# Pooling bands moved in the load queue, gate rows and weight loads tied to later work in a two-block transformer kernel

## The chip, the cores and the metric

The kernel runs on one core of a Trainium2 chip. A core has a matrix engine (TensorE, PE in the profile, with PEld for its weight loads), a vector engine (VectorE, DVE), a scalar engine (ScalarE, ACT), GpSimd (POOL) and a sync engine (SyncE, SP) that here does nothing but issue loads. Each engine runs its own list of instructions in the order in which they are written and waits on semaphores. 16 DMA engines carry the loads. Loads that SP issues, those that ACT issues and those that POOL issues form three queues (q1, q10 and q0). The metric is the device time of one execution in microseconds (us); lower is better.

## The reference, cut to what matters

Two transformer blocks of two layers each run on 256 tokens of 1024 features, all in float32. The changed code is in the first layer of the first block:

```python
def sandwich(x, mod, g_pre, g_post, fn):
    shift, scale, gate = mod                     # split(silu(c) @ ada_w + ada_b, 3)
    h = rms_norm(x, g_pre) * (1.0 + scale[:, None]) + shift[:, None]
    return x + gate[:, None] * rms_norm(fn(h), g_post)

def mixer(h, j=j):                               # layer 0
    u, qr, fr, vr, gr = jnp.split(h @ hyb_w_in[j], split_at, axis=-1)
    y = jnp.concatenate([pool_mixer(u, pool_w[j], pool_scale[j]),
                         hgrn2_mixer(qr, fr, vr, gr, lower_bounds[j], hgrn_out_norm[j])], axis=-1)
    return y @ hyb_w_out[j]
```

`pool_mixer` takes a windowed mean over the tokens minus the token itself (in the kernel a matmul with a table of bands), then a 128x128 weight per group. `hgrn2_mixer` is a gated linear recurrence with q = silu(q_raw); the kernel computes it by levels that double in length. Behind the mixer come a feed-forward layer (swiglu), then the second layer (dilated attention, swiglu), then the second block.

## The kernel before, in words

Each float32 weight matmul is done as three products of a high and a low part. Weights come in loads of 1 MB into a ring of six slots (`raw`). A load has two halves; the `split` of ACT casts a half to its high part (`whi`, L587), the `split` of DVE subtracts it (`wlo`, L1373, which raises `lo_ready`), and TensorE multiplies. There are four slots of high and low parts.

The start, up to about 147 us of the profile, is made of these steps:

- Eight modulation chunks of 1 MB and four loads of hyb_w_in (half of which hold two blocks each) alternate in SP's queue. DVE makes the shift and scale of the first norm from the chunks; each chunk done raises `ada_used`. TensorE multiplies block 0 (pooling inputs u) and block 1 (the forget gate) as eight tiles.
- Six loads n4 to n9 (hyb_in 4 to 9) hold blocks 2 (query), 3 and 4 with halves 8 to 19; four loads n10 to n13 hold hyb_w_out with halves 20 to 27; n14 is the first load of the feed-forward layer with halves 28 and 29. In the code, `split(2 * FIRST["hyb_in"] + 14 + i)` is half 14 + i.
- TensorE runs halves 8 and 9, then the eight pooling matmuls with `bandqk` (which wait for `band_in`, raised by the bands and by `poolw`, and for the copy of block 0 out of PSUM), halves 10 and 11, then eight levels of the recurrence with one half ahead of each.
- ACT copies the blocks out of PSUM (`evac`), makes sigmoids and Silu, prepares keys, and in each level makes the level copies (L922, L923), which DVE's next level and TensorE's scores wait for.
- DVE makes the query product `QG` (L1793), the level products, the masked merges (`copy_predicated` with `masks`) and the splits; between them stand items of work on rows: 8 gate items (`gate_items(0, ...)`, one row of the gate weights of the first mixer each) and 16 items of the second modulation (`col_items(1, ...)`). Each item raises `ada_step`.
- POOL issues the rows, 0.5 MB each, into a ring of four (`ada_ring`); a row is issued once the item four places back is done. The first gate row waits for `ada_used`.
- Two semaphore waits of SP hold back the loads. Load n of 4 to 13 waits for `lo_ready` of 2 * (n - EARLY) + 2, and n14 waits for the count of one of the four row semaphores:

```python
if isinstance(it, int) and max(EARLY, len(HYB_AT)) <= n < FIRST["ffn0"]:
    sp.wait_ge(s["lo_ready"], 2 * (n - EARLY) + 2)
...
sp.wait_ge(ada_in[3], 16 * 5)
```

The fourth row semaphore (`ada_in[3]`) counts rows 3, 7, 11, 15, 19 and 23 of the whole sequence; the rows 8 to 23 of that sequence are rows 0 to 15 of the second modulation.

Of the kernel before, what the change touches and what calls it, by code (L numbers as in the profile page):

```python
# [47 lines left out]
FIRST, _n = {}, 0  # L48
ADA_FIRST = 8
# [1 line left out]
HYB_AT = (1, 4, 7, 10)  # L51
ROW_STEP = 1
GATE_ITEMS, COL_ITEMS = (0, 24, 48, 72), (None, 8, 32, 56)
EARLY = 3
for _name, _k in PHASES:
    FIRST[_name] = _n
    _n += _k
# [35 lines left out]
def program(nc, t):  # L93

    with ExitStack() as ctx:
        s = {name: ctx.enter_context(nc.semaphore(name)) for name in SEMS}
        raw_in = [s[f"raw_in{i}"] for i in range(RAW)]
        ada_in = [s["ada_in0"], s["ada_in1"], s["ada_in2"], s["ada_in3"]]
# [95 lines left out]
        def flat(bank, n=2):  # L194
            return ps[:, bank:bank + n, :].rearrange("p a b -> p (a b)")
# [192 lines left out]
        def _(sp):  # L388
# [35 lines left out]
            def proj(n, w, blocks, it=0, step=0):  # L424
                for b, (_, col0, _) in enumerate(blocks):
                    for kh in range(2):
                        load(n + 2 * b + kh, it, src_cols(w, col0 + step * it, kh))
# [26 lines left out]
            for at in range(ADA_FIRST + len(HYB_AT)):  # L454
# [3 lines left out]
                    load_both(HYB_AT.index(at))  # L458
                if at == 2:
                    sp.dma_start(voh[:, :], t["voh"]).then_inc(s["const_in"], 16)  # L460
            proj(FIRST["hyb_in"] + 4, t["hyb_w_in"][0], HYB[2:])
            for c in range(4):
                load(FIRST["hyb_out"] + c, 0, src_down(t["hyb_w_out"][0], c * 2 * P))
            sp.wait_ge(ada_in[3], 16 * 5)
            swiglu(FIRST["ffn0"], 0)
            with sp.Fori(0, 2) as i:
                proj(FIRST["qkv"], t["att_w_qkv"][0], QKV_B, i, 1536)
# [23 lines left out]
        def _(pool):  # L491
# [33 lines left out]
            pool.memset(gg[:, :, :], 0.0).then_inc(s["gg_zero"], 1)  # L525
            bias_row(0)
            bias_row(1)
            pool.wait_ge(s["ada_used"], ADA_FIRST - 1)
            gate_rows(0, range(8))
            gain_row(0)  # L530
            mod_rows(1, range(16))
# [43 lines left out]
        def _(act):  # L575
            A = nc.scalar

            def split(H, it=0):

                if isinstance(it, int) and H >= HALVES:  # L580
                    return
                n, h = H // 2, H % 2
                if h == 0:
                    act.wait_ge(raw_in[slot(n)], in_count(n) + 16 * it)
                if H >= 4:
                    act.wait_ge(s["pe_used"], H - 3 + 12 * it)
                A.copy(whi[:, H % 4, :], raw[:, slot(n), h * HALF:(h + 1) * HALF]).then_inc(s["hi_ready"], 1)  # L587
# [261 lines left out]
            for k in range(KD):  # L849
                split(k)  # L850
                if k == 5:
                    table_row(0)
                    table_row(1)
                if k == 7:
                    act.dma_start(bandqk[:, :], t["band"]).then_inc(s["band_in"], 16)
                    act.dma_start(poolw[:, :, :], t["pool_w"][0].rearrange("g c d -> c g d")).then_inc(s["band_in"], 16)
                if k == 0:
                    act.wait_ge(s["turned"], KD)
                act.wait_ge(s["mod_ready"], k + 1)
                if k >= 4:  # L860
                    act.wait_ge(s["hlo_ready"], k - 3)
                A.activation(h32_slot(0, k), turned_ps(0, k), ACT.Identity, bias=shcol[:, 0, k:k + 1],
                             scale=scol[:, 0, k:k + 1])
                A.activation(hhi[:, k, :], turned_ps(0, k), ACT.Identity, bias=shcol[:, 0, k:k + 1],
                             scale=scol[:, 0, k:k + 1]).then_inc(s["hhi_ready"], 1)
                if k == 6:
                    table_row(2)
                    act.wait_ge(s["vec_dil"], 3 + DG)
                    A.copy(vrow[:, 3 * VLEN_DIL:], ps[0:8, 5, :]).then_inc(s["vec_dil_c"], 1)
                    act.wait_ge(s["vec_dil_c"], 4)  # L870
                    act.dma_start(t["vec_dil"].rearrange("g h n -> h g n"),
                                  vrow[:, 0:3 * VLEN_DIL].rearrange("h (g n) -> h g n", g=3)).then_inc(s["vec_out"], 16)
                    act.dma_start(t["vec_swa"], vrow[:, 3 * VLEN_DIL:]).then_inc(s["vec_out"], 16)
# [3 lines left out]
            fl = f1[:, :, :].rearrange("p a b -> p (a b)")  # L877
            split(8)
            split(9)
            evac(0, KD, "A", HYB[0][2], f1, tok1)  # L880
            act.dma_start(masks[:, :, :], t["masks"]).then_inc(s["cols_in"], 16)
            evac(1, KD, "B", HYB[1][2], f1, tok1)
            split(10)
            split(11)
            act.wait_ge(s["vec_out"], 32)
            act.wait_ge(s["proj_free"], 2)
# [9 lines left out]
            for h in range(HL):  # L896
# [2 lines left out]
                ins = A.activation(fl[:, 1024 + a:1024 + a + S], fl[:, 1024 + a:1024 + a + S], ACT.Identity,  # L899
                                   bias=small[:, 4, h:h + 1], scale=small[:, 4, 4 + h:5 + h])  # L900
            ins.then_inc(s["hg_prep"], 1)
            evac(2, 2 * FIRST["hyb_in"] + 12, HYB[2][0], HYB[2][2], f1, tok1)
            act.wait_ge(s["proj_free"], 3)
            A.activation(fl[:, 0:1024], fl[:, 0:1024], ACT.Silu).then_inc(s["sig_ready"], 1)
            A.copy(pooled[:, :, :].rearrange("p a b -> p (a b)"), flat(6)).then_inc(s["pool_dc"], 1)
            split(13)
            split(14)
            split(15)
# [448 lines left out]
        def _(dve):  # L1357
# [244 lines left out]
            def proj(name, blocks, at=0, it=0):  # L1602
                for b in range(len(blocks)):
                    for q in range(4):
                        split(2 * (FIRST[name] + 2 * (at + b)) + 4 + q, it)
# [181 lines left out]
            split(11)  # L1787
            gate_items(0, acc_a, (1,))
            split(12)
            gate_items(0, acc_a, (2, 3))  # L1790
            dve.wait_ge(s["hg_prep"], 1)
            dve.wait_ge(s["sig_ready"], 3)
            V.tensor_tensor(QG, fl[:, 0:1024], fl[:, 1024:2048], ALU.mult).then_inc(s["hg_prep"], 1)  # L1793
            gate_items(0, acc_a, (4,))
            split(13)
            split(14)

# [39 lines left out]
            for i in range(8):  # L1837
                if i:
                    level(i)
                if 0 <= i - 1 < 5:  # L1840
                    merge(i - 1)
                if i:
                    split(2 * FIRST["hyb_in"] + 14 + i)
                if 1 <= i <= 3:
                    gate_items(0, acc_a, (i + 4,))
                elif 4 <= i <= 6:
                    col_items(1, (i - 4,))
                if i == 7:
                    dve.wait_ge(s["hyb_hi"], 1)
                    V.tensor_tensor(hlo[:, 0:4, :], y1[:, 0:4, :], hhi[:, 0:4, :].bitcast(F32), ALU.subtract) \  # L1850
                        .then_inc(s["hyb_lo"], 1)
            split(2 * FIRST["hyb_in"] + 22)
            col_items(1, (3, 4))
            split(2 * FIRST["hyb_in"] + 23)
            col_items(1, (5, 6))
            split(2 * FIRST["hyb_out"] + 4)
            col_items(1, (7, 8))
            dve.wait_ge(s["sig_ready"], 4)
            for c in range(2):
                yv = y1[:, 4 + 2 * c:6 + 2 * c, :].rearrange("p a b -> p (a b)")  # L1860
# [7 lines left out]
                V.tensor_tensor(hlo[:, 4 + 2 * c:6 + 2 * c, :], y1[:, 4 + 2 * c:6 + 2 * c, :],  # L1868
                                hhi[:, 4 + 2 * c:6 + 2 * c, :].bitcast(F32), ALU.subtract).then_inc(s["hyb_lo"], 1)
            split(2 * FIRST["hyb_out"] + 5)  # L1870
            col_items(1, (9, 10))
            split(2 * FIRST["hyb_out"] + 6)
            col_items(1, (11,))
            split(2 * FIRST["hyb_out"] + 7)
            col_items(1, (12, 13))
            whole_gate(0, 2)
            col_items(1, (14, 15))
            split(2 * FIRST["hyb_out"] + 8)
            renew(1)
            split(2 * FIRST["hyb_out"] + 9)  # L1880
# [1393 lines left out]
```

## Time and profile before

| | |
|---|---|
| Time, median of 3 runs | 1264.63 us (1264.23 to 1266.15) |
| The profiled execution | 1264.12 us, span 1262.3 us |
| TensorE busy | 1233.4 us, 98% of the span |
| VectorE busy | 920.2 us, 73% |
| ScalarE busy | 721.1 us, 57% |
| Mean granted TensorE clock | 0.995 of full speed |
| HBM read | 272.30 MB, 217 GB/s over the span |

The busy shares are averages over all stages. In the first 150 us the three compute engines and the queues have other shares than later, and the change is there.

### The profile page before, as it was taken

How to read it: one execution, taken by the hardware profiler on the slowest of the kernel's cores; microseconds unless marked ns; L12 is line 12 of the kernel's file. 1: busy time of each engine (PE TensorE's matmuls, PEld its weight loads, DVE VectorE, ACT ScalarE, POOL GpSimd, SP SyncE). 2: the span in 40 equal slices, each digit the busy share in tenths (PEclk: the TensorE clock that was granted, in tenths of full speed). 3: DMA queues.
4: the chain of work that ended last, by engine and by line, in shares of the span. 5: the costliest groups of instructions: out<-in, count | busy, mean ns of one | idle time of the engine just before them, and what ended most of it. 6: DMA issues, size and time to landing. Idle time of an engine off the chain costs nothing.

```text
span 1262.3 us, 20465 instructions
## 1 busy us (share of the span) xinstructions
PE 1233.4 (98%) x7874; PEld 1118.5 (89%) x7874; DVE 920.2 (73%) x1193; ACT 721.1 (57%) x1062; POOL 63.1 (5%) x116
## 2 busy tenths in 40 slices
PE   8799899999999999999999999999999999999999
PEld 6698799999899778999989989888888888888888
DVE  7779878886897558666676695676666777766665
ACT  5676644444744557444466664665555667655554
POOL 1101111110121000000001000000000000000000
PEclk9999899999999999999999999999999999999999
DMA  9967989995699624666656544356666552466650
GB/s 362 395 223 254 340 304 328 330 331 195 242 384 392 210 48 167 200 200 199 199 167 214 165 152 151 131 201 201 201 205 202 188 171 92 131 214 203 200 167 34
DMA packets 145903, 274.39 MB, mean 217 GB/s; under 512 B 5463, under 2 KB 86383, under 8 KB 145704
## 3 DMA queue, kind: packets, MB, share of 16 engines
q1 hardware_dynamic: 130524, 220.50, 51.8%
q0 software_dynamic: 14256, 50.94, 11.4%
q10 hardware_dynamic: 1052, 1.97, 0.4%
q8 instruction: 48, 0.79, 0.3%
q14 instruction: 23, 0.19, 0.0%
HBM read 272.30 MB, written 1.10 MB: 217 GB/s over the span
## 4 chain that ended last, share of the span: by engine, by line
PE 86%; DVE 6%; DMA 3%; ACT 2%; issue 2%; SPq 0%; ACTq 0%; DVEq 0%
PE ps L2321 85%; DVE wlo L1373 2%; DMA raw<-in_hyb_w_in 1%; DMA poolw<-in_pool_w 1%; ACT whi L587 1%; PE ps L2763 1%; DVE raw L1401 1%; DMA ada_ring<-in_ada_t 1%; DVE ada_ring L1401 0%; DVE h L1476 0%; DVE x L1485 0%; PE ps L2487 0%; PE ps L2500 0%; DVE rs L2041 0%; DVE prob L1998 0%
## 5 line engine op out<-in xcount | busy, mean ns | idle before, releaser
L1373 DVE TENSOR_TENSOR wlo<-raw,whi 128x1024 fp32r<-128x1024 f32 x400 | 488.4, 1227 | 241.0 <-ACT whi L587 240.3
L587 ACT CAST whi<-raw 128x1024 fp32r<-128x1024 f32 x400 | 417.3, 1050 | 402.3 <-PE ps L2321 386.9
L2321 PE MATMUL ps<-hboth,whi 128*128 128x256 f32 (+1 forms) x2720 | 605.3, 311 | 0.7 <-DVE hboth L1597 0.2
L2321 PE MATMUL ps<-hboth,wlo 128*128 128x256 f32 x1792 | 491.3, 274 | 0.6 <-DVE wlo L1373 0.2
L2321 PEld LDWEIGHTS ps<-hboth,whi 128*128 128x128 f32 x2720 | 448.0, 191 | 29.9 <-issue 5.3
L2321 PEld LDWEIGHTS ps<-hboth,wlo 128*128 128x128 f32 x1792 | 344.2, 192 | 2.9 <-issue 1.0
L2321 PE MATMUL ps<-whi,hboth 128*128 128x512 f32 (+1 forms) x520 | 158.0, 374 | 9.3 <-DVE hboth L1427 7.1
L2321 PE MATMUL ps<-whi,hidhi 128*128 128x512 f32 (+1 forms) x436 | 164.8, 378 | 0.0
L2321 PE MATMUL ps<-wlo,hidhi 128*128 128x512 f32 (+1 forms) x436 | 164.4, 377 | 0.0
L2321 PE MATMUL ps<-whi,hidlo 128*128 128x512 f32 (+1 forms) x436 | 164.4, 377 | 0.0
L2321 PEld LDWEIGHTS ps<-whi,hboth 128*128 128x128 f32 x520 | 96.8, 190 | 26.6 <-issue 12.8
L2321 PE MATMUL ps<-wlo,hboth 128*128 128x512 f32 (+1 forms) x260 | 94.9, 365 | 0.0
L2321 PEld LDWEIGHTS ps<-wlo,hidhi 128*128 128x128 f32 x436 | 82.5, 189 | 11.5 <-issue 0.2
L2321 PEld LDWEIGHTS ps<-whi,hidlo 128*128 128x128 f32 x436 | 82.4, 189 | 11.5
L2321 PEld LDWEIGHTS ps<-whi,hidhi 128*128 128x128 f32 x436 | 82.6, 189 | 10.5 <-ACT whi L587 0.2
L1401 DVE CUSTOM_DVE_ANT_0 ada_ring<-ada_ring,scrow,cols 128x1024 f32<-128x1024 f32 x48 | 61.0, 1291 | 1.7 <-DMA ada_ring<-in_ada_t 1.5
L2321 PEld LDWEIGHTS ps<-wlo,hboth 128*128 128x128 f32 x260 | 49.5, 190 | 6.0 <-issue 1.0
L1720 DVE TENSOR_REDUCE tmp<-ps 128x512 f32<-128x1024 f32 x32 | 39.0, 1219 | 3.5 <-PE ps L2321 3.5
L1725 DVE TENSOR_TENSOR hidlo<-hid,hidhi 128x512 fp32r<-128x512 f32 x32 | 22.2, 692 | 16.7 <-ACT hidhi L810 16.7
L496 POOL DMA_DIRECT2D ada_ring<-in_ada_t x48 | 25.4, 530 | 134.7 <-DVE shcol L1401 63.6
L1394 DVE SCALAR_TENSOR_TENSOR acc_a<-ada_ring,sc,acc_a 128x1024 f32<-128x1024 f32 x21 | 27.3, 1298 | 0.5
L496 POOL DMA_DIRECT2D ada_ring<-in_ada_w x32 | 17.0, 531 | 140.0 <-DVE scol L1401 61.4
(271 smaller groups left out, 1120.7 us busy)
## 6 DMA issues: line engine op xcount, KB each, us to landing
raw<-in_ffn_w_in SPq DMA_DIRECT2D x44, 1024.0 KB, 5.5
raw<-in_w_mlp_up SPq DMA_DIRECT2D x32, 1024.0 KB, 5.3
raw<-in_w_mlp_down SPq DMA_DIRECT2D x32, 1024.0 KB, 4.9
ada_ring<-in_ada_t POOLq DMA_DIRECT2D x48, 512.0 KB, 6.0
raw<-in_ffn_w_out SPq DMA_DIRECT2D x22, 1024.0 KB, 4.9
raw<-in_att_w_qkv SPq DMA_DIRECT2D x18, 1024.0 KB, 8.9
raw<-in_w_in_even SPq DMA_DIRECT2D x18, 1024.0 KB, 5.1
ada_ring<-in_ada_w POOLq DMA_DIRECT2D x32, 512.0 KB, 6.5
```

The source lines that it names most:

```text
L496: pool.dma_start(ada_ring[:, l % 4, :], src).then_inc(ada_in[l % 4], 16)
L587: A.copy(whi[:, H % 4, :], raw[:, slot(n), h * HALF:(h + 1) * HALF]).then_inc(s["hi_ready"], 1)
L1373: V.tensor_tensor(wlo[:, H % 4, :], raw[:, slot(n), h * HALF:(h + 1) * HALF], whi[:, H % 4, :].bitcast(F32), ALU.subtract).then_inc(s["lo_ ...
L1394: ins = V.scalar_tensor_tensor(out=acc[:, :], in0=row, scalar=sc[:, k:k + 1], in1=acc[:, :], op0=ALU.mult, op1=ALU.add)
L1401: return V.tensor_tensor_reduce(out=row, in0=row, in1=scrow[:, :], scale=1.0, scalar=col(name, 8 * j + k), op0=ALU.mult, op1=ALU.add, accu ...
L1720: V.tensor_reduce(in_order(tmp2[:, g % 3, :], 2), parts_of(UP_BANK[g % 3]), AX, ALU.add) \
L1725: V.tensor_tensor(hidlo2[:, g % 3, :], hid2[:, g % 3, :], hidhi2[:, g % 3, :].bitcast(F32), ALU.subtract).then_inc(s["mhid_lo"], 1)
L2321: return pe.matmul(out, lhsT, rhs, start=first, stop=last, skip_group_check=True)
L2763: m = pe.transpose(dl_turned(p, i)[:, (j - j0) * P:(j - j0 + 1) * P], dl_block(p, j), ident[:, :])
```

## The change

The diff does seven things: (1) the loads of the bands and of pool_w go from ACT's queue to SP's, directly behind the last modulation chunk; (2) the load of the masks goes from ACT's queue to SP's, behind n5; (3) EARLY is 2 in place of 3; (4) n14 waits for a count of 6 rows in place of 5; (5) POOL's first gate row waits for eight chunks used in place of seven; (6) ACT casts half 10 ahead of the copies of blocks 0 and 1, and makes the pooled copy ahead of the copy of block 2 and of the Silu; (7) DVE has gate items 2 to 5 ahead of the query product and item 6 behind it, and all later items of the second modulation two places earlier, with `whole_gate` behind the last of them.

```diff
-EARLY = 3
+EARLY = 2
@@ sync
-            proj(FIRST["hyb_in"] + 4, t["hyb_w_in"][0], HYB[2:])
+            sp.dma_start(bandqk[:, :], t["band"]).then_inc(s["band_in"], 16)
+            sp.dma_start(poolw[:, :, :], t["pool_w"][0].rearrange("g c d -> c g d")).then_inc(s["band_in"], 16)
+            proj(FIRST["hyb_in"] + 4, t["hyb_w_in"][0], HYB[2:3])
+            sp.dma_start(masks[:, :, :], t["masks"]).then_inc(s["cols_in"], 16)
+            proj(FIRST["hyb_in"] + 6, t["hyb_w_in"][0], HYB[3:])
...
-            sp.wait_ge(ada_in[3], 16 * 5)
+            sp.wait_ge(ada_in[3], 16 * 6)
@@ gpsimd
-            pool.wait_ge(s["ada_used"], ADA_FIRST - 1)
+            pool.wait_ge(s["ada_used"], ADA_FIRST)
@@ scalar
-                if k == 7:
-                    act.dma_start(bandqk[:, :], t["band"]).then_inc(s["band_in"], 16)
-                    act.dma_start(poolw[:, :, :], t["pool_w"][0].rearrange("g c d -> c g d")).then_inc(s["band_in"], 16)
...
             split(9)
+            split(10)
             evac(0, KD, "A", HYB[0][2], f1, tok1)
-            act.dma_start(masks[:, :, :], t["masks"]).then_inc(s["cols_in"], 16)
             evac(1, KD, "B", HYB[1][2], f1, tok1)
-            split(10)
...
             ins.then_inc(s["hg_prep"], 1)
+            A.copy(pooled[:, :, :].rearrange("p a b -> p (a b)"), flat(6)).then_inc(s["pool_dc"], 1)
             evac(2, 2 * FIRST["hyb_in"] + 12, HYB[2][0], HYB[2][2], f1, tok1)
...
-            A.copy(pooled[:, :, :].rearrange("p a b -> p (a b)"), flat(6)).then_inc(s["pool_dc"], 1)
@@ vector
-            gate_items(0, acc_a, (2, 3))
+            gate_items(0, acc_a, range(2, 6))
...
-            gate_items(0, acc_a, (4,))
+            gate_items(0, acc_a, (6,))
...
-                if 1 <= i <= 3:
-                    gate_items(0, acc_a, (i + 4,))
-                elif 4 <= i <= 6:
-                    col_items(1, (i - 4,))
+                if i == 1:
+                    gate_items(0, acc_a, (7,))
+                elif 2 <= i <= 6:
+                    col_items(1, (i - 2,))
...
             split(2 * FIRST["hyb_out"] + 5)
-            col_items(1, (9, 10))
+            col_items(1, (11, 12))
             split(2 * FIRST["hyb_out"] + 6)
-            col_items(1, (11,))
+            col_items(1, (13,))
             split(2 * FIRST["hyb_out"] + 7)
-            col_items(1, (12, 13))
+            col_items(1, (14, 15))
             whole_gate(0, 2)
-            col_items(1, (14, 15))
```

What stands on ACT before, from the cast of half 8 to the sigmoids (L587 is a cast, tok is block 0, f is block 1):

```order
L587 CAST whi<-raw 128x1024 [waits pe_used,raw_in0]
L587 CAST whi<-raw 128x1024 [waits pe_used]
L597 COPY tok<-ps 128x2x512 [waits pe_used]
L881 DMA masks<-in_masks 128x1024
L595 COPY f<-ps 128x1024 [waits pe_used]
L587 CAST whi<-raw 128x1024 [waits pe_used,raw_in1]
L587 CAST whi<-raw 128x1024 [waits pe_used]
L887 ACT_TABLE_LOAD [waits proj_free]
L887 ACTIVATE sq<-f 128x1024 [waits vec_out]
```

And in the changed kernel (L591 is the cast there):

```order
L591 CAST whi<-raw 128x1024 [waits pe_used,raw_in0]
L591 CAST whi<-raw 128x1024 [waits pe_used]
L591 CAST whi<-raw 128x1024 [waits pe_used,raw_in1]
L601 COPY tok<-ps 128x2x512 [waits pe_used]
L599 COPY f<-ps 128x1024 [waits pe_used]
L591 CAST whi<-raw 128x1024 [waits pe_used]
L887 ACT_TABLE_LOAD [waits proj_free]
L887 ACTIVATE sq<-f 128x1024 [waits vec_out]
```

The cast that waits for n5 (`raw_in1`) stands now ahead of the two copies of blocks, and the load of the masks is gone from ACT.

What stands on SP in the changed kernel from the last modulation chunk to the first feed-forward load:

```order
L400 DMA raw<-in_ada_t 128x2x1024 [waits ada_used]
L461 DMA bandqk<-in_band 128x2048
L462 DMA poolw<-in_pool_w 128x4x128
L422 DMA raw<-in_hyb_w_in 128x4x512 [waits ada_used,lo_ready]
L422 DMA raw<-in_hyb_w_in 128x4x512 [waits lo_ready]
L464 DMA masks<-in_masks 128x1024
L422 DMA raw<-in_hyb_w_in 128x4x512 [waits ada_used,lo_ready] x2
L422 DMA raw<-in_hyb_w_in 128x4x512 [waits lo_ready]
L422 DMA raw<-in_hyb_w_in 128x4x512 [waits ada_used,lo_ready]
L422 DMA raw<-in_hyb_w_out 128x2x1024 [waits lo_ready] x4
L422 DMA raw<-in_ffn_w_in 128x8x256 [waits lo_ready,ada_in3]
```

Before, the loads of hyb_w_in followed each other without the three rows of L461, L462 and L464; the values waited for are in the diff.

What stands on DVE before, behind the last low part ahead of the hyb_out halves (L1401 is an item of the second modulation, L1451 is `whole_gate`):

```order
L1868 TENSOR_TENSOR hboth<-y,hboth 128x512 [waits hyb_hi] x2
L1373 TENSOR_TENSOR wlo<-raw,whi 128x1024 [waits hi_ready]
L1401 ISA ada_ring,scol<-ada_ring,scrow,cols 128x1024 [waits ada_in1]
L1401 ISA scol 128x1
L1401 ISA ada_ring,scol<-ada_ring,scrow,cols 128x1024 [waits ada_in2]
L1401 ISA scol 128x1
L1373 TENSOR_TENSOR wlo<-raw,whi 128x1024 [waits hi_ready]
L1401 ISA ada_ring,scol<-ada_ring,scrow,cols 128x1024 [waits ada_in3]
L1401 ISA scol 128x1
```

And in the changed kernel at the same place:

```order
L1868 TENSOR_TENSOR hboth<-y,hboth 128x512 [waits hyb_hi] x2
L1373 TENSOR_TENSOR wlo<-raw,whi 128x1024 [waits hi_ready]
L1401 ISA ada_ring,scol<-ada_ring,scrow,cols 128x1024 [waits ada_in3]
L1401 ISA scol 128x1
L1401 ISA ada_ring,scol<-ada_ring,scrow,cols 128x1024 [waits ada_in0]
L1401 ISA scol 128x1
L1373 TENSOR_TENSOR wlo<-raw,whi 128x1024 [waits hi_ready]
L1401 ISA ada_ring,scol<-ada_ring,scrow,cols 128x1024 [waits ada_in1]
```

The items behind half 25's low part are 9 and 10 before (rows of the semaphores `ada_in1` and `ada_in2`) and 11 and 12 now (`ada_in3` and `ada_in0`).

## Rows read from the trace of the kernel before

**Rows 1.** The page: the span, and TensorE's busy time and share.

```profile
span 1262.3 us, 20465 instructions
PE 1233.4 (98%) x7874; PEld 1118.5 (89%) x7874; DVE 920.2 (73%) x1193; ACT 721.1 (57%) x1062; POOL 63.1 (5%) x116
```

**Rows 2.** Waits of TensorE: us in total, times, longest.

```profile
PE ps L2487 <- DVE xn L1523: 6.9, 3, 5.3
PE ps L2321 <- DMA poolw<-in_pool_w: 4.2, 1, 4.2
```

**Rows 3.** The chain that ended last: start, us, what.

```profile
146.66 73.52 PE ps L2321 x572
```

**Rows 4.** Window: length, busy of PE, PEld, DVE, ACT, POOL, clock, DMA, GB/s.

```profile
57.10:62.20 5.10, 5.04 (x17) 4.19 (x17) 3.70 (x3) 2.69 (x3) 1.49 (x3) 0.67 1.04 398
```

**Rows 5.** Timeline of SP and POOL: start, us, what is issued.

```profile
28.28 0.47 SPq L400 DMA_DIRECT2D raw<-in_ada_t  x1
...
73.73 0.37 SPq L422 DMA_DIRECT2D raw<-in_hyb_w_in  x1
...
117.28 0.53 POOL L496 DMA_DIRECT2D ada_ring<-in_ada_t  x1 [2.13 <-DVE shcol L1401]
...
121.81 1.07 SPq L422 DMA_DIRECT2D raw<-in_ffn_w_in  x2
```

**Rows 6.** DMA issues at 28, at 72 and from 75: KB, us to landing.

```profile
raw<-in_ada_t SPq DMA_DIRECT2D x1, 1024.0 KB, 11.4
...
raw<-in_hyb_w_in SPq DMA_DIRECT2D x1, 1024.0 KB, 6.2
...
raw<-in_hyb_w_out SPq DMA_DIRECT2D x3, 1024.0 KB, 5.0
```

**Rows 7.** Queues in windows 41-42, 43-44, 130-131: packets, MB, engine share.

```profile
q1 hardware_dynamic: 194, 0.39, 105.4%
...
q0 software_dynamic: 71, 0.29, 73.3%
...
q0 software_dynamic: 84, 0.31, 80.0%
q1 hardware_dynamic: 85, 0.09, 24.5%
```

**Rows 8.** ACT: a window as in rows 4, then its timeline.

```profile
50.88:70.03 19.15, 14.98 (x94) 13.64 (x94) 8.46 (x7) 13.40 (x18) 2.64 (x5) 0.91 0.94 352
...
68.97 1.06 ACT L904 ACTIVATE f<-f 128x1024 f32<-128x1024 f32 x1
...
76.86 0.85 ACT L923 COPY sq<-bandqk 128x512 f32<-128x512 f32 x1
...
104.01 1.01 ACT L595 COPY f<-ps 128x1024 f32<-128x1024 f32 x1 [0.78 <-PE ps L2321]
...
128.19 2.23 ACT L587 CAST whi<-raw 128x1024 fp32r<-128x1024 f32 x2 [4.67 <-DMA raw<-in_ffn_w_in]
```

**Rows 9.** Timeline of DVE: start, us, what, idle before and who ended it.

```profile
70.14 1.23 DVE L1793 TENSOR_TENSOR bandqk<-f 128x1024 f32<-128x1024 f32 x1 [8.75 <-ACT f L904]
...
80.69 1.00 DVE L1832 TENSOR_TENSOR bandqk<-pooled,tot 128x512 f32<-128x512 f32 x1
...
98.06 1.44 DVE L1401 CUSTOM_DVE_ANT_0 ada_ring<-ada_ring,scrow,cols 128x1024 f32<-128x1024 f32 x1
...
106.00 1.23 DVE L1850 TENSOR_TENSOR hboth<-y,hboth 128x1024 fp32r<-128x1024 f32 x1 [0.45 <-ACT hboth L947]
...
124.61 1.28 DVE L1401 CUSTOM_DVE_ANT_0 ada_ring<-ada_ring,scrow,cols 128x1024 f32<-128x1024 f32 x1
...
132.10 1.28 DVE L1401 CUSTOM_DVE_ANT_0 ada_ring<-ada_ring,scrow,cols 128x1024 f32<-128x1024 f32 x1 [1.53 <-DMA ada_ring<-in_ada_t]
...
139.64 0.75 DVE L1485 SCALAR_TENSOR_TENSOR x<-h,small,x 128x512 f32<-128x512 f32 x1
...
143.89 0.75 DVE L1523 TENSOR_SCALAR xn<-x,small 128x1024 f32<-128x1024 f32 x1
```

More of the change, by code:

```diff
@@ L1852, in _ @@
             split(2 * FIRST["hyb_in"] + 22)
-            col_items(1, (3, 4))
+            col_items(1, (5, 6))
             split(2 * FIRST["hyb_in"] + 23)
-            col_items(1, (5, 6))
+            col_items(1, (7, 8))
             split(2 * FIRST["hyb_out"] + 4)
-            col_items(1, (7, 8))
+            col_items(1, (9, 10))
             dve.wait_ge(s["sig_ready"], 4)
```

## The prediction

> **What bounds the kernel now.** I read the page first: TensorE is busy for 98% of the span of 1262.3 us [rows 1], so time can only come from its few idle stretches or go into new ones. Then its waits: one of 4.2 us for the pooling weights and one of 5.3 us for the normalised x ahead of the first feed-forward stage [rows 2]. Everything the change touches ends before 147 us, and behind that point the chain that ends last stays on TensorE for 73.5 us on end [rows 3], so whatever shift the first feed-forward stage receives is carried to the end one for one. Then the windows: in 57.1 to 62.2, with the eight pooling matmuls, TensorE has a granted clock of 0.67, a mixture of its two levels (1.2 and 2.4 GHz), after the 4.2 us of standing idle [rows 4]. Last, the queues and the other two engines, which run in written order: a load that is late stops ScalarE (ACT) at its cast, and all that is written behind the cast waits too.
>
> Names: n4 to n13 are the one-block weight loads of SP (six of hyb_w_in, four of hyb_w_out), n14 is the first of ffn_w_in. Load n holds halves 2n and 2n+1, each cast by ACT and then subtracted by VectorE (DVE).
>
> **Part 1: bands and pooling weights ahead of n4.** The last modulation chunk was issued at 28.28 and landed 11.4 us later, at 39.7; the queue of SP is that deep [rows 5, 6]. Alone, that queue moves 0.39 MB per us [rows 7], window 41 to 42. Behind it stand now the bands (1.05 MB, 2.7 us), pool_w (0.26 MB, 0.7 to 0.9 us) and n4 (1.05 MB, 2.7 us): n4 lands at 45.9. Two passes (a cast of 1.05 on ACT, a subtraction of 1.15 on DVE) make its half 8 ready at 48.2, about when TensorE has finished the eighth tile: no more than 0.4 us lost. The pooling inputs land at 43.3, well ahead.
>
> But TensorE's pooling also needs the copy of PSUM block 0, and ACT now makes it behind the cast of half 10, so behind n5. From 39.7 on the engines must move the bands, pool_w, n4, four gate rows (4 x 0.52 MB, which start about 46) and n5: 5.5 MB at 0.39 is 14.1 us, so n5 lands at 53.8. That does not hang on how the two queues share, because the row queue takes 0.29 of 0.39 when both have work [rows 7], window 43 to 44, and is finished first. The cast (1.0 us) and copy (1.0 us) put pooling at 55.9, against 57.2 before; bounds 54.5 (rows late) and 56.5.
>
> The next thing late is ACT's query Silu, which the query product on DVE needs. From the cast of half 10 to the end of the Silu took 19.15 us before (50.88 to 70.03), with 13.4 us of work and the rest idle for a load and for TensorE [rows 8]; 13.5 with the small gaps. Now three copies more stand in that piece (blocks 0 and 1, and the pooled copy moved ahead of the Silu), 1.0 us each: 16.5 us. 53.8 and 16.5 is 70.3. The product started at 70.14 before [rows 9]. So the 4.2 us wait shrinks, and the slow clock behind it may go (5.04 us busy at 0.67 is 3.4 at full clock, some 1.6 us), but what follows from them is given back at once: the query product starts at the old time. Value of part 1: 0, between -0.8 (n5 at 53.0) and +0.5. The two further gate items moved into DVE's 8.75 us idle ahead of the product cost nothing there, since their rows (issued behind items 0 and 1, near 58 and 61) have until 69 to land; the masks are needed behind the first level and land behind n5, at 55.
>
> **Part 2: EARLY 3 to 2.** Each of n4 to n13 now waits for one load more to be split: n waits for half 2n-3 to be subtracted, before for half 2n-5. n8 was issued behind half 11; now it is issued behind half 13, where n9 was: 73.73. A load issued just there took 6.2 us with one row beside it, others 5.0 [rows 5, 6]. So n8 lands at 79.9 (78.8 to 80.2). Behind the cast of its half 16 (1.05 us) stand ACT's level copies 1 (1.7 us), the second of which ended at 77.7 before [rows 8]; now at 82.6. DVE's level 2 needs them and started at 80.69 [rows 9]: DVE is late by 1.9 us (0.8 to 2.2). DVE has no idle time of its own from there to half 21, so it keeps that. TensorE's levels had some 2 us in hand over DVE's merges and are late by 1.1.
>
> n11 is issued behind half 19 now, which ended where the next item begins, at 98.06 [rows 9], and ends at 100.0 (plus 1.9). It lands at 105.1 (5.0 us) or 106.2. What ACT has in its row then: cast of half 22 (1.0), level copies 7 (1.2), merge 6 (0.7), copy of block 4 (1.0): 109.0. The copy of block 4 ended at 105.0 before [rows 8] and the low part of the first four feature tiles, two steps behind, began at 106.00 [rows 9]. Late by 4.0 us, bounds 2.5 (1.9 replaced by 0.8, 5.0 kept) and 5.2. n10, n12 and n13 are late too, but stop ACT where nothing is waited for.
>
> **Part 3: the gate row count 5 to 6.** The rows and items of the second modulation are numbered 0 to 15 as in the code. n14 waits now for row 15, before for row 11. A row is issued when the item four places back is done. Row 11 followed item 7, and n14 was issued at 121.81 [rows 5]. From the issue of row 11 at 117.28 (0.4 behind the end of item 7) to n14's issue it took 4.5 us. Row 15 follows item 11, which now stands where item 9 stood, so ends at 124.61 [rows 9] plus 4.0 = 128.6. With the same 0.4 and 4.5, n14 is issued at 133.5.
> It landed 6.4 us after issue, when ACT's cast began at 128.19 [rows 8] and the row queue stood still for most of it. Now the four rows of the next gate and a gain row are issued beside it. When both have work, the row queue takes 0.31 MB per us and the 1 KB pieces of ffn_w_in 0.09, with 84 and 85 pieces each [rows 7], window 130 to 131; that would make it 10.3. I take 7.5, since the row queue has gaps of over 1 us between rows: 141.0. The Trainium skill, page "DMA: Bandwidth & Descriptors", section "Queues, rings and completion order", says that an engine takes turns between queues by whole packets of typically 9 to 17 descriptors; its section on SWDGE and HWDGE prefers packets up to 4096 B. Bytes would then be shared evenly, n14 would take about 6.5 and the time be 1 us less. The trace shows equal numbers of pieces and unequal bytes, so the sum goes by the trace.
>
> ACT has n14's two casts (2.2 us) ahead of the squares of y. Two squares (1.6) and the root (0.5) follow, 4.4 us with the gaps, then DVE's update of x, which before began at 139.64, and 4.25 us later the normalisation at 143.89 [rows 9]. So normalisation starts at 141.0 + 4.4 + 4.25 = 149.7: late by 5.8 us. Without the new wait DVE would have reached it at 143.9 even with the 4.0 us of part 2, because two modulation items fewer stand in that stretch (2.4 us) and the 1.53 us wait for a row [rows 9] goes. So the 4.0 and the 5.8 aren't added: the chain through the row, n14 and ACT contains the 4.0 and takes DVE's saving away. Bounds: with part 2 at 2.5 and n14 in 5.0 us it is 5.8 - 1.5 - 2.5 = 1.8; with part 2 at 5.2 and n14 in 10.3 it is 5.8 + 1.2 + 2.8 = 9.8.
>
> **Sum.** The profiled execution took 1264.12 us, span 1262.3. Plus 5.8 is 1269.9; the median of the runs stands 0.5 above the profiled one: 1270.4.
>
> **Rivals.**
> A, faster: n5 lands early enough that the copy of block 0 is not held up, by 50 or so. Then pooling runs at 53.4, TensorE is 5 us ahead, the query Silu comes some 3 us earlier, and DVE goes into the levels that much sooner. Every later load is tied to DVE's progress and moves too; with the two items fewer at the end it would be 3 to 4 us faster: 1261. It decides on n5's landing: below 51. Against it: 3.3 us too many bytes stand ahead of n5.
> B, no change: the late loads stop ACT but the waits die in slack, and n14 lands as fast as before (row queue idle). DVE's own row then sets the end: 0 to 1 us late, 1265.4. For it: DVE's path alone gives 0. Against it: ACT's casts stand ahead of the copies and squares in written order.
> C, worse: the waits at the levels and at hyb_out let the clock fall to 1.2 GHz, as after the 4.2 us at 57 [rows 4]; another 1.6 us as there, and n14 at its slow bound (2.8): 1274.8.
>
> **Chances.** Forecast 0.62 (own range 1267.3 to 1273), A 0.11, B 0.17, C 0.10. A measurement here can tell about 0.2%, 2.5 us. Faster by more than that: A, 0.10. Within: B, the edge of A and the low edge of the forecast, 0.20. Slower: 0.70. The 8-in-10 range takes B and most of C in: 1264.5 to 1274.
>
> **What would show it.** Right: no wait of TensorE for poolw, but one of 2 to 3 us at the same matmul put down to the copy of block 0; the query product at 70 to 71; ACT idle for hyb_w_in at half 16 (about 4 us) and for hyb_w_out at half 20 and 22; TensorE waiting 2 to 3 us near 107; ACT idle for ffn_w_in until about 141; the wait for the normalised x at 7 to 9 us. Wrong: level copies 1 finished before 80, or n14 landing before 137. If the pooling matmuls start before 54.5, step 1 is wrong and A gains.

## The result, and the profile after

The changed kernel takes 1276.39 us (median of 4 runs, 1275.4 to 1277.84) against 1264.64 us: the ratio is 1.0092, with a 95% interval of 1.0074 to 1.0109. The forecast was 1270.4. The profiled execution after took 1275.4 us with a span of 1273.5 us, against 1264.12 and 1262.3 [rows 1].

The page of the changed kernel, the span and the busy time of the engines:

```profile
span 1273.5 us, 20465 instructions
PE 1234.9 (97%) x7874; PEld 1119.9 (88%) x7874; DVE 920.6 (72%) x1193; ACT 718.1 (56%) x1062; POOL 62.9 (5%) x116
```

The busy time is the same within 2 us on every engine but ACT (3 us less), and the span is 11.2 us longer. The difference stands in waits. The waits of TensorE in the changed kernel, as in [rows 2]:

```profile
PE ps L2486 <- DVE xn L1523: 11.8, 3, 10.2
...
PE ps L2320 <- DVE wlo L1373: 3.8, 4, 1.7
PE ps L2320 <- ACT tok L601: 2.5, 1, 2.5
PE ps L2320 <- ACT sq L923: 1.8, 1, 1.8
```

The wait for the pooling weights has gone, and in its place stands one of 2.5 us for the copy of block 0 (`tok`), as forecast. The wait for the normalised x grew from 5.3 to 10.2 us, and small ones were added at the levels. The chain that ended last, as in [rows 3], from the hyb_out halves on:

```profile
109.23 0.02 ACT f L599
...
111.22 1.23 DVE hboth L1850
...
116.29 7.56 DMA ada_ring<-in_ada_t
...
130.46 1.20 DVE ada_ring L1401
131.67 0.28 issue
131.95 3.74 DMA ada_ring<-in_ada_t
135.71 11.72 DMA raw<-in_ffn_w_in
147.45 1.99 ACT whi L591 x2
...
155.91 0.68 DVE xn L1523
...
166.54 3.47 PE ps L2320 x29
```

It is the path of part 3, step by step: item 11 ends at 131.67, row 15 is issued and lands in 3.74 us, n14 is issued at 135.71 and takes 11.72 us, ACT casts it, and 8.4 us behind the landing x is normalised. On the timeline of DVE, as in [rows 9], all that went late is seen in turn:

```profile
70.71 1.22 DVE L1793 TENSOR_TENSOR bandqk<-f 128x1024 f32<-128x1024 f32 x1 [1.03 <-ACT f L905]
...
83.31 0.69 DVE L1832 TENSOR_TENSOR bandqk<-pooled,tot 128x512 f32<-128x512 f32 x1 [2.13 <-issue]
...
111.22 1.23 DVE L1850 TENSOR_TENSOR hboth<-y,hboth 128x1024 fp32r<-128x1024 f32 x1 [2.21 <-ACT hboth L947]
...
123.87 1.29 DVE L1401 CUSTOM_DVE_ANT_0 ada_ring<-ada_ring,scrow,cols 128x1024 f32<-128x1024 f32 x1 [1.67 <-DMA ada_ring<-in_ada_t]
...
155.82 0.75 DVE L1523 TENSOR_SCALAR xn<-x,small 128x1024 f32<-128x1024 f32 x1
```

Against [rows 9] the query product is late by 0.6, level 2 by 2.6, the low part ahead of hyb_out by 5.2, and the normalisation by 11.9 us (155.82 against 143.89). The span grew by 11.2: that shift, less 0.7 us that was not traced. The other three runs are up to 2.4 us longer than the profiled one; they left no traces.

### The profile page after: what moved, and what is told of

It reads as the page before. It is cut to its first block, busy times and chain, and to the rows that moved or that the text cites. A ratio compares the mean times of both kernels' runs of the same rounds, so it can differ in the third digit from the quotient of the medians.

```text
span 1273.5 us, 20465 instructions
## 1 busy us (share of the span) xinstructions
PE 1234.9 (97%) x7874; PEld 1119.9 (88%) x7874; DVE 920.6 (72%) x1193; ACT 718.1 (56%) x1062; POOL 62.9 (5%) x116
## 3 DMA queue, kind: packets, MB, share of 16 engines
q1 hardware_dynamic: 131340, 222.34, 51.7%
## 4 chain that ended last, share of the span: by engine, by line
PE 83%; DVE 6%; DMA 4%; ACT 4%; issue 2%; SPq 0%; ACTq 0%; DVEq 0%
PE ps L2320 82%; DMA raw<-in_hyb_w_in 3%; DVE wlo L1373 2%; ACT whi L591 1%; DMA raw<-in_ffn_w_in 1%; DMA ada_ring<-in_ada_t 1%; PE ps L2762 1%; DVE raw L1401 1%; DVE h L1476 0%; DVE x L1485 0%; PE ps L2486 0%; PE ps L2499 0%; DVE ada_ring L1401 0%; DVE rs L2040 0%; DVE prob L1997 0%
## 5 line engine op out<-in xcount | busy, mean ns | idle before, releaser
L591 ACT CAST whi<-raw 128x1024 fp32r<-128x1024 f32 x400 | 416.7, 1048 | 430.4 <-PE ps L2320 386.4
L2320 PEld LDWEIGHTS ps<-whi,hboth 128*128 128x128 f32 x520 | 97.7, 192 | 31.6 <-issue 16.5
L1401 DVE CUSTOM_DVE_ANT_0 ada_ring<-ada_ring,scrow,cols 128x1024 f32<-128x1024 f32 x48 | 60.6, 1280 | 1.9 <-DMA ada_ring<-in_ada_t 1.9
```

What stands on the lines that cost most here:

```text
L1401: return V.tensor_tensor_reduce(out=row, in0=row, in1=scrow[:, :], scale=1.0, scalar=col(name, 8 * j + k), op0=ALU.mult, op1=ALU.add, accu ...
L2320: return pe.matmul(out, lhsT, rhs, start=first, stop=last, skip_group_check=True)
```

## The experiments

Theory 1 is the path just read: EARLY 2 makes the weight loads late, the count of 6 puts n14 behind row 15, and the rows of the next gate that POOL issues beside n14 lengthen its landing. Its rivals are told with each run. All ratios are to the kernel before on the same chip, with 95% intervals. Its medians there were 1264.39 us (for the first four kernels below), 1265.14 (the next four), 1264.29 (the next two) and 1264.22 (the last).

**The count back to 5.**

```diff
-            sp.wait_ge(ada_in[3], 16 * 6)
+            sp.wait_ge(ada_in[3], 16 * 5)
```

> The changed kernel with n14's wait for row 11 again (count 5), all else as changed. Theory 1 (two costs: the loads tied one further back make the recurrence about 5 us late, and the count of 6 makes n14 land at 147.4, about 6 us more): n14 is issued at about 125.5 behind row 11 and lands by 137, so the normalised x comes at about 147 in place of 155.8; time 1267 to 1269. Theory 2 (the count costs nothing, all of it is EARLY): stays at 1276. Theory 3 (it is the count alone): back to 1264 or below.

1267.42 us (1265.76 to 1271.49), ratio 1.0024 (1.0014 to 1.0034). n14 is issued at 127.26 in place of 135.71 and x is normalised 7.0 us earlier:

```profile
148.82 0.75 DVE L1523 TENSOR_SCALAR xn<-x,small 128x1024 f32<-128x1024 f32 x1
```

So both costs of theory 1 are there. The count is worth 0.68% here (1.0092 against 1.0024) and 0.69% when it alone is added to the kernel before (below). It is not the largest single cost in the changed kernel: EARLY put back alone gives 0.82% (next).

**EARLY back to 3.**

```diff
-EARLY = 2
+EARLY = 3
```

> The changed kernel with EARLY 3 again, count still 6. Theory 1: halves 16, 20 and 22 are cast without a wait for their loads, the first hyb_out half starts at about 107.4 in place of 112.6, n14 is issued near 129 and still takes about 11 us, the normalised x comes at about 149; time 1269 to 1271. Theory 2 (EARLY is all of it): 1263 to 1265. Theory 3 (the count is all of it): stays at 1276.

1266.13 us (1261.92 to 1268.81), ratio 1.001 (0.9997 to 1.0023): better than expected by 3 us, and spread over 7 us. Two lines of ACT show one reason. The cast that waits for n5, in the changed kernel:

```profile
54.64 1.04 ACT L591 CAST whi<-raw 128x1024 fp32r<-128x1024 f32 x1 [6.55 <-DMA raw<-in_hyb_w_in]
```

And with EARLY 3:

```profile
51.93 1.05 ACT L591 CAST whi<-raw 128x1024 fp32r<-128x1024 f32 x1 [3.55 <-DMA raw<-in_hyb_w_in]
```

EARLY acts on n4 and n5 too; I had priced it only from n8 on. With EARLY at 2, n5 waits for the low part of half 7 and is issued at 44.20; with EARLY at 3 it waits for half 5 and is issued at 38.96, and it lands 2.7 us earlier. With EARLY 3 the pooling matmuls don't wait at all and the query product starts at 68.16, 2 us ahead of the kernel before. In this trace n14 is issued at 126.00 and takes 7.89 us. The spread is taken up below.

**Both back.**

```diff
-EARLY = 2
+EARLY = 3
...
-            sp.wait_ge(ada_in[3], 16 * 6)
+            sp.wait_ge(ada_in[3], 16 * 5)
```

> The changed kernel with EARLY 3 and count 5, so that only the order of loads, the casts and the items is changed. Theory 1: both costs are gone and what is left is the saving of two modulation items behind the hyb_out halves and of a part of the pooling wait, 0 to 3 us faster than before: 1262 to 1264.6. A rival (the moved bands themselves delay the loads, and ACT's earlier cast of half 10 costs as much as it brings) gives 1266 to 1269.

1259.18 us (1258.22 to 1259.49), ratio 0.9953 (0.9936 to 0.9969). This is faster than the kernel before by 5.2 us, and beyond what was expected. The waits of TensorE there:

```profile
PE ps L2320 <- DVE hboth L1427: 8.8, 6, 1.8
PE ps L2486 <- DVE xn L1523: 4.7, 3, 3.1
```

Neither the pooling weights nor block 0 is waited for, and x is normalised 5.2 us earlier than in [rows 9]:

```profile
138.67 0.75 DVE L1523 TENSOR_SCALAR xn<-x,small 128x1024 f32<-128x1024 f32 x1
```

What is left of the change (the moved loads, the later gate rows, the order of ACT and the items that DVE does earlier) is a gain here; beside EARLY 2 the forecast had put part 1 at nothing.

**The rows of the next gate held back until n14 is split.**

```diff
+            pool.wait_ge(s["lo_ready"], 29)
             gate_rows(1, range(4))
```

> The changed kernel, with POOL's eight rows of the second gate held back until n14's first half is split, so that n14 has the DMA engines to itself. If the 11.7 us that n14 took come from sharing with those rows (theory 1, the term of the sum that was mis-sized), n14 lands in 5 to 6.5 us, the normalised x comes some 5.5 us earlier, time 1270 to 1271.5. If n14 is slow by itself, or the four loads issued one behind another slow each other, it stays at 1275 to 1277.

1268.87 us (1268.04 to 1270.68), ratio 1.0034 (1.0021 to 1.0046): 7.5 us less than the changed kernel, and 1.1 below the expected range. The profiled run is the one of 1270.68; against the profiled run of the changed kernel it is 4.7 us shorter, with x normalised at 150.16, 5.7 earlier. The chain here, at the same place:

```profile
131.53 3.82 DMA ada_ring<-in_ada_t
135.37 6.39 DMA raw<-in_ffn_w_in
141.78 1.99 ACT whi L592 x2
```

n14 is issued within 0.4 us of the same time and takes 6.39 us in place of 11.72. Nothing else was edited, so the rows beside it are what made it slow. The queues between issue and landing of n14 (packets, MB, share of the 16 engines), first in the changed kernel, 135.71 to 147.43:

```profile
q0 software_dynamic: 675, 2.46, 60.3%
q1 hardware_dynamic: 1572, 1.59, 39.3%
```

and with the rows held back, 135.37 to 141.76:

```profile
q1 hardware_dynamic: 1704, 1.73, 81.9%
```

In the changed kernel the row queue was busy in two stretches, up to about 140 and again from about 142. By 142.7 the queue of SP had already moved 1.11 MB, more than the 1.05 MB of n14, and n14 was not complete: a part of these bytes belongs to n15, which stands right behind it in that queue. How n14 fell behind is inferred: some of the 16 engines seem to have been ahead with n15 while others still had last pieces of n14, and these met the next rows. The changed kernel again, 142.7 to 147.4:

```profile
q0 software_dynamic: 373, 1.35, 73.6%
q1 hardware_dynamic: 472, 0.48, 29.6%
```

In 4.7 us the queue of SP moved 0.10 MB per us, where it moves 0.35 to 0.37 alone.

**The count of 6 alone, in the kernel before.**

```diff
-            sp.wait_ge(ada_in[3], 16 * 5)
+            sp.wait_ge(ada_in[3], 16 * 6)
```

> The kernel before with the count of the gate row wait at 6 alone. Theory 1 (n14 is issued some 3.8 us behind row 15, and lands late because its last pieces meet the burst of gate rows): row 15 went at 128.53, so n14 is issued at 132.3. If its tail meets the burst it takes 11.7 us as in the changed kernel, lands at 144.0, and x is normalised 8.4 us later, at 152.4, late by 8.5: 1273. If it takes 7.9 us as in the changed kernel with EARLY 3, it is 1269. Expected 1269 to 1273. Rival (the count costs little by itself and only bites with the late loads): 1264 to 1266.

1273.56 us (1269.27, 1273.41, 1273.7 and 1274.35), ratio 1.0069 (1.0052 to 1.0086), 0.6 above the expected range. The profiled run is the one of 1269.27; its chain:

```profile
127.81 4.67 DMA ada_ring<-in_ada_t
132.49 8.13 DMA raw<-in_ffn_w_in
140.64 1.99 ACT whi L587 x2
```

There n14 took 8.13 us and x was normalised at 149.02, late by 5.1, as the time is. The other three runs are 4 to 5 us longer. That would be the difference between a landing of 8 and one of 12 us; they left no traces, so this is not shown.

**EARLY 2 alone, in the kernel before.**

```diff
-EARLY = 3
+EARLY = 2
```

> The kernel before with EARLY 2 alone. Theory 1 (late levels and hyb_out, the two modulation items left in the stretch behind, n14 lands in 7.6 us as with the count of 5): like the changed kernel with the count of 5, x normalised 4 to 5 us late: 1267 to 1269. Rival (the costs of the parts add up: the changed kernel less the changed kernel with EARLY 3 is 10.3 us): 1274.

1268.54 us (1267.13 to 1270.1), ratio 1.0032 (1.0019 to 1.0044), within the expected range. x is normalised at 148.25. The start of this trace has something that no theory named. n5 is issued at 44.55 in place of 35.69, behind the bands that ACT issues at 42.21, and the pooling matmuls wait only 0.87 us for the pooling weights (4.2 before): they start at 54.10, and the query product at 68.94, 1.2 us ahead of [rows 9]. So EARLY 2 shortens the pooling wait by itself, and what it costs comes behind that.

**EARLY 3 in the changed kernel, with the rows held back.**

```diff
-EARLY = 2
+EARLY = 3
...
+            pool.wait_ge(s["lo_ready"], 29)
             gate_rows(1, range(4))
```

> The changed kernel with EARLY 3, and the rows of the next gate held back until n14 is split (low part of half 28 done). Theory 1 (the runs of the kernel with EARLY 3 spread from 1261.9 to 1268.8 because the last pieces of n14 sometimes meet the burst of gate rows): with no row beside it n14 takes 6.4 us, x is normalised at 140.8, the time is 1260.5 to 1262.5 and the runs lie within 2.5 us of each other. Rival (the spread comes from something else): median 1264 to 1267, still spread over 5 us or more.

1260.18 us (1259.99 to 1260.97), ratio 0.9962 (0.9948 to 0.9976). The runs lie within 1.0 us of each other, where they were 6.9 us apart without the hold, and the median fell by 6. So the spread was made by the rows beside n14, as theory 1 said. In the trace ACT's cast of n14 starts 5.4 us behind its issue and waits for TensorE, no longer for the load.

**The cast of half 10 back behind the copies of blocks 0 and 1**, beside EARLY 3 and the count of 5:

```diff
-            split(10)
             evac(0, KD, "A", HYB[0][2], f1, tok1)
             evac(1, KD, "B", HYB[1][2], f1, tok1)
+            split(10)
```

> The changed kernel with EARLY 3 and the count of 5 (1259.2), with ACT's cast of half 10 back behind its copies of blocks 0 and 1. Theory 1: ACT's two copies (1.9 us) move into its wait of 3.7 us for n5, and from n5's landing to the query Silu ACT has no gap, so the query product starts 1.9 us earlier and the end follows: 1257 to 1258. Rival (DVE or a load sets the levels instead): within 0.7 of 1259.2.

1258.37 us (1257.12 to 1259.37), ratio 0.9946 (0.9929 to 0.9962), not to be told from 1259.18. The mechanism of theory 1 fell: the query product started at 68.24, against 67.82 without the edit. The cast of n4 was 0.55 us late in this trace too (46.58 against 46.03), so the product is neither early nor late against it. ACT's copies did move into its wait, but the next load was late in their place. Its casts of halves 10 and 11 and of half 12:

```profile
52.36 2.02 ACT L591 CAST whi<-raw 128x1024 fp32r<-128x1024 f32 x2 [1.96 <-DMA raw<-in_hyb_w_in]
...
58.25 1.05 ACT L591 CAST whi<-raw 128x1024 fp32r<-128x1024 f32 x1 [1.51 <-DMA raw<-in_hyb_w_in]
```

**EARLY 2 and the count of 6 in the kernel before**, so without part 1 and the moved items:

```diff
-EARLY = 3
+EARLY = 2
...
-            sp.wait_ge(ada_in[3], 16 * 5)
+            sp.wait_ge(ada_in[3], 16 * 6)
```

> The kernel before with EARLY 2 and the count of 6, the bands and pooling weights left on ACT's queue: the changed kernel without part 1 and without the moved items. Theory 1 (with EARLY 2 the load n5 is issued 5 us later, which takes back all that part 1 could give, so part 1 is worth nothing beside it): 1275 to 1278, as the changed kernel. Rival (part 1 is worth its 5 us here too): 1280 to 1283.

1274.32 us (1272.33 to 1275.32), ratio 1.0082 (1.0065 to 1.0099), 0.7 below the expected range. The changed kernel has 1.0092: beside EARLY 2 and the count of 6, all the rest of the change gives nothing that can be measured. Beside EARLY 3 and the count of 5 the same edits gave 5.2 us. Two lines of this trace show that the nothing is made of more than one piece:

```profile
PE ps L2321 <- DMA poolw<-in_pool_w: 1.5, 1, 1.5
...
67.51 1.23 DVE L1793 TENSOR_TENSOR bandqk<-f 128x1024 f32<-128x1024 f32 x1 [3.81 <-ACT f L904]
```

The wait for the pooling weights is down to 1.5 us without any load moved, and the query product starts 3.2 us ahead of the changed kernel (70.71). There the cast of half 10 starts at 54.64, here at 54.15; from that cast to the product it takes 16.1 us there and 13.4 here, and the changed kernel has three more copies of ACT in between (blocks 0 and 1, and the pooled copy), about 1 us each. Yet n14 is issued at 135.28 here and at 135.71 there, so the changed kernel wins nearly all of it back behind the product. ACT's old order was not tried by itself beside EARLY 2.

**The two loads alone moved, in the kernel before.**

```diff
-                if k == 7:
-                    act.dma_start(bandqk[:, :], t["band"]).then_inc(s["band_in"], 16)
-                    act.dma_start(poolw[:, :, :], t["pool_w"][0].rearrange("g c d -> c g d")).then_inc(s["band_in"], 16)
...
+            sp.dma_start(bandqk[:, :], t["band"]).then_inc(s["band_in"], 16)
+            sp.dma_start(poolw[:, :, :], t["pool_w"][0].rearrange("g c d -> c g d")).then_inc(s["band_in"], 16)
             proj(FIRST["hyb_in"] + 4, t["hyb_w_in"][0], HYB[2:])
```

> The kernel before with the bands and pooling weights alone moved to SP's queue ahead of n4; all engines' orders, EARLY 3 and the count of 5 as before. Theory 1 (the moved loads end the wait for the pooling weights, n5 lands near 52 and the query product starts near 68.3 in place of 70.1): 1.8 us go at the query product, 1261 to 1263. Rival (what the changed kernel with EARLY 3 and the count of 5 gains, 5 us, comes from the gate and modulation items that DVE does earlier): 1264 to 1265.5.

1266.26 us (1264.55 to 1267.87), ratio 1.0017 (1.0008 to 1.0027). Theory 1 missed, and the rival is nearer: no gain at all, but a small loss. The wait of TensorE had only changed its name:

```profile
PE ps L2320 <- DVE wlo L1372: 4.5, 3, 4.0
```

n4 was cast at 49.30, against 46.03 with EARLY 3 and the count of 5. The difference is in POOL. In this kernel the four gate rows start as before:

```profile
38.80 2.10 POOL L498 DMA_DIRECT2D ada_ring<-in_ada_w  x4 [33.92 <-DVE scol L1400]
```

and between 41 and 49 they move 1.55 MB, as much as SP's queue:

```profile
q1 hardware_dynamic: 909, 1.54, 53.7%
q0 software_dynamic: 415, 1.55, 48.8%
```

**The two loads moved and the gate rows later.** The edit before, and with it:

```diff
-            pool.wait_ge(s["ada_used"], ADA_FIRST - 1)
+            pool.wait_ge(s["ada_used"], ADA_FIRST)
```

> The kernel before with bands and pooling weights on SP's queue ahead of n4, and the gate rows begun one modulation item later (at 42.6 in place of 38.8); nothing else. In the kernel with the loads alone n4 was cast at 49.3, since from 41 on the rows took most of the engines. Theory 1 (the later rows are what lets n4 land by 46, and with that the moved loads pay): n4 cast near 46.4, query product near 68.3, 1.8 us earlier than before, time 1261.5 to 1263; the rest of the gain of the changed kernel with EARLY 3 and the count of 5 (1259.2) is then the items that DVE does earlier. Rival (the rows' start doesn't matter): 1265.5 to 1267, like the kernel with the loads alone.

1261.98 us (1260.56 to 1263.43), ratio 0.9979 (0.9969 to 0.9989). Theory 1 holds. The rows start at 43.06, and from 41 to 49 the queues move:

```profile
q1 hardware_dynamic: 1330, 2.32, 80.0%
q0 software_dynamic: 201, 0.76, 23.8%
```

n4 is cast at 45.97, the query product starts at 66.88 and x is normalised at 140.83, 3.1 us earlier than before. One line of a wait made the difference between a loss of 0.17% and a gain of 0.21%. The further 2.8 us to 1259.18 come with what the fuller kernel has beside it: the masks in SP's queue, the order of ACT and the items of DVE moved ahead. They were not taken apart. In the traces the query product starts 0.9 us later in the fuller kernel (67.82 against 66.88) and x is normalised 2.2 us earlier (138.67 against 140.83), so the gain arises behind the product.

The eight kernels that have EARLY, the count and all the rest of the change (numbers 1, 2, 5, 6 and 7 of the list in the section on the change) or not, as ratio to before:

| | EARLY 3, count 5 | EARLY 3, count 6 | EARLY 2, count 5 | EARLY 2, count 6 |
|---|---|---|---|---|
| the rest as before | 1 | 1.0069 | 1.0032 | 1.0082 |
| the rest as changed | 0.9953 | 1.001 | 1.0024 | 1.0092 |

The first two columns differ from row to row by 0.5 to 0.6%, the last two by 0.1% in either direction: the rest of the change is worth 5 to 6 us beside EARLY 3 and nothing beside EARLY 2. The traces give three parts of the reason; no run takes them apart. EARLY 2 makes n5 late whether the loads are moved or not (its cast starts at 54.15 to 55.85 in the four kernels of these columns, at 50.88 before); it shortens the pooling wait by itself where they are not moved; and ACT's new order puts three copies between n5 and the query product.

## Why the prediction was wrong in its size

The sign and the path were right: the chain through the row, n14 and ACT sets the end. The forecast shift of the normalised x was 5.8 us and the measured one 11.9, so the time came out at 1276.39, above the range of 1264.5 to 1274. The step that failed is the time that n14 takes to land. By the steps:

- **Part 1.** n4 at 45.9 (cast at 46.10), n5 at 53.8 (54.64), the pooling matmuls at 55.9 (56.65), the query product at 70.1 to 70.3 (70.71), no wait for `poolw` and one of 2.5 us for block 0 in its place: all as forecast, each up to 0.8 late, and the value of nothing beside EARLY 2 is borne out by the two columns of the table. But the nothing is partly luck. The prediction counted bytes ahead of n5 and said that this "does not hang on how the two queues share", by which n5 would be as late for any EARLY. It named the wait for "n4 to n13" and then priced it only from n8 on. The sum of 5.5 MB has all four gate rows ahead of n5, and they are ahead only because EARLY 2 issues n5 (44.20) behind them (42.73; forecast near 46). The queues from 44 to 48, in the changed kernel:

```profile
q0 software_dynamic: 348, 1.30, 84.5%
q1 hardware_dynamic: 87, 0.15, 10.1%
```

and with EARLY 3 and the count of 5:

```profile
q1 hardware_dynamic: 546, 1.15, 76.0%
q0 software_dynamic: 99, 0.41, 25.6%
```

  In both kernels the engines are full; what differs is whose bytes go first, and n5 lands 2.7 to 2.9 us earlier. So rival A was ruled out by a count of bytes that holds for EARLY 2 alone. Its steps came true once EARLY was back at 3 and the count at 5 (pooling at 53.93, product 2.3 us earlier, 1259.2 for its 1261), though n5 landed at 51.7 and not below 51. They did not come true in the kernel with only the loads moved, where the early gate rows made n4 late. The three copies of ACT were in the sum, as 16.5 us from n5 to the Silu, and measured 16.0.
- **Part 2.** n8 landed at 81.1, not 79.9 (the cast's start is taken for the landing); the level was late by 2.6, not 1.9; hyb_out was late by 5.2, not 4.0, at the upper bound of 5.2. n8 was issued near 74.3, since the product was late by 0.6, and took 6.8 us.
- **Part 3, the issue of n14.** Item 11 began 7.0 us later than item 9 had before; 4.0 was forecast. 1.2 of that is part 2, and 1.7 a wait for a row at 123.87 that the prediction hadn't: with the items two places further on, rows are needed sooner behind the late hyb_out. From the end of item 11 to the issue of n14 it took 4.1 us, 0.8 less than forecast. n14 was issued at 135.7, 2.2 late on 133.5.
- **Part 3, the landing of n14: the step that failed.** The prediction saw the split of the queues [rows 7], worked out 10.3 us from it, and then took 7.5 "since the row queue has gaps of over 1 us between rows". It took 11.7, beyond even the 10.3, whose working the prediction doesn't write out. The gaps are there, and by 142.7 SP's queue had moved 1.1 MB, mostly in one of them; n14 was complete only 4.7 us later, with the row queue busy again. With the rows held back it takes 6.4, so the sharing with the rows is shown; that it was the last pieces that met them is inferred. The even share of bytes, which gave 6.5, is not borne out: from 142.7 to 147.4 the queues moved 373 and 472 pieces, and 1.35 against 0.48 MB. The Trainium skill, page "DMA: Bandwidth & Descriptors", section "Queues, rings and completion order", says only that an engine takes turns by whole packets, typically of 9 to 17 descriptors; the even bytes were the prediction's own step from the two sections that it names. Packets of as many descriptors on either side would give about equal pieces, so this trace does not contradict the page.
- **Behind n14.** 8.4 us from landing to normalisation, 8.65 forecast.

The sum: 5.8, and 2.2 for the issue, 4.2 for the landing, less 0.3 behind it, is 11.9. Two thirds of the miss are the landing.

Of the rivals, C had the slow bound of n14 in it, was given 0.10, and its 1274.8 was the nearest; that it came so near is partly luck, since n14 was slower than its bound and its 1.6 us for the clock have no place in the sum above. B fell: DVE's own path did not set the end. The slower clock that C named is there (0.91 in 72 to 108, where the kernel before has 1.00); what it cost by itself was not measured. The windows of the changed kernel, columns as in [rows 4]:

```profile
53.00:58.00 5.00, 2.50 (x15) 2.10 (x14) 2.28 (x2) 3.36 (x4) 0.00 (x0) 0.90 0.75 281
58.00:63.00 5.00, 5.00 (x23) 4.26 (x23) 3.77 (x5) 4.95 (x6) 1.05 (x2) 0.75 0.61 199
...
72.00:108.00 36.00, 33.35 (x233) 31.16 (x232) 33.01 (x47) 19.69 (x33) 3.70 (x7) 0.91 0.68 230
...
130.00:147.00 17.00, 14.71 (x87) 12.99 (x85) 10.06 (x15) 0.49 (x1) 3.16 (x6) 1.00 0.78 270
147.00:165.00 18.00, 8.38 (x61) 8.32 (x62) 13.91 (x28) 14.78 (x39) 0.00 (x0) 0.72 1.00 331
```

In 130 to 147 ACT is busy for 0.49 us: the whole engine stands in front of one cast. In 53 to 63 the clock was mixed again (0.90 and 0.75) in spite of the shorter wait, so the 1.6 us that might have been won there were not. The pooling matmuls show it, in the changed kernel and, without any wait ahead of them, with EARLY 3 and the count of 5:

```profile
56.65 5.41 PE L2320 MATMUL ps<-bandqk,tok 128*128 128x256 f32 x16 [2.50 <-ACT tok L601]
...
53.93 3.62 PE L2320 MATMUL ps<-bandqk,tok 128*128 128x256 f32 x16
```

They took 5.38 us in the kernel before: behind a wait of 2.5 us they were as slow as behind one of 4.2, and without a wait they were 1.8 us faster, at a granted clock of 1.00.

## What to carry to other kernels

When a load moves ahead of others, find every wait that holds back the loads behind it, and the other queues that start in the same stretch: here the same two moved loads were worth a loss of 0.17% or a gain of 0.21%, by when the gate rows start, and the whole bundle around them 0.5% or nothing, by how far SP may run ahead. A load whose landing is on the path ends with its last piece, and its mean rate can mislead: if another queue issues bursts in the time that it needs, take the slow share for its end, and look for a run-to-run spread of that size. The best version here keeps the new place of the loads, the later gate rows and the moved items, and leaves EARLY at 3 and the count at 5: 1259.18 us, 0.47% faster than before. With the cast of half 10 at its old place it took 1258.37, which is not to be told from that.

## What the runs showed of the hardware that was not expected

- The same 1 MB load n14, in pieces of 1 KB, took 6.4 us with the row queue idle (at most 5.4 with EARLY 3), and 7.9, 8.1, 9.2 and 11.7 us with almost the same rows issued beside it (EARLY 3; the count of 6 alone; both in the kernel before; the changed kernel). In the two kernels for which the spacing was compared (EARLY 3 and the changed kernel), the rows stood at -2.5, -0.2, +2.1 to 2.2, +3.3 to 3.4 and +4.7 us from n14's issue (the last one is the short gain row), yet one took 7.9 and the other 11.7.
- A load was complete only when its queue had moved 1.27 to 1.73 MB from its issue on, though it has 1.05 MB: pieces of the loads behind it went ahead of its own last ones. That the engines drift apart is inferred from these sums; no view showed the single engine.
